# Expert rows gathered on TensorE by one fp32 product per tile in place of two products with split rows

## The reference, cut to what matters

```python
h2 = rmsnorm(x, norm2_g) * (1.0 + scale2) + shift2
# router: softmax over 16 experts, best group of 4, best two experts in it
combine = ...                                   # (tokens, 16), two nonzero per token
hidden = silu(einsum('td,edf->tef', h2, w_gate)) * einsum('td,edf->tef', h2, w_up)
hidden = hidden * combine[:, :, None]
x = x + gate2 * einsum('tef,efd->td', hidden, w_down)
```

## Time and profile before

| | |
|---|---|
| median of 3 runs | 897.79 us (896.08 to 898.65) |
| profiled execution, its own time | 893.21 us |
| its span in the trace | 891.4 us |
| PE busy | 803.2 us (90%) |
| DVE busy | 614.2 us (69%) |
| ACT busy | 432.1 us (48%) |
| DMA, mean over the span | 196 GB/s |

### The profile page before, as it was taken

How to read it: one execution, slowest core, us unless ns; L and a number is a source line. 1 busy time by engine, 2 the same in 40 slices (tenths; PEclk the granted TensorE clock), 3 DMA queues, 4 the chain that set the end, 5 groups by cost and what they waited for, 6 DMA issues and landing times.

```text
span 891.4 us, 10532 instructions
## 1 busy us (share of the span) xinstructions
PE 803.2 (90%) x3988; PEld 640.1 (72%) x3988; DVE 614.2 (69%) x739; ACT 432.1 (48%) x504; POOL 73.3 (8%) x67
## 2 busy tenths in 40 slices
PE   1239999999999979999999759999999999999993
PEld 0028878787666646667888758888888888888882
DVE  3685895122699986553654863979788888888882
ACT  1323214245655545556221634656657575756660
POOL 4020000000000000000000000011111121111111
PEclk9959999999999999999999758999999999999998
DMA  9918958020111131132273251989898989989873
GB/s 317 332 55 323 344 192 314 0 77 19 48 41 56 47 95 48 48 133 81 95 261 142 92 201 60 326 266 347 313 343 309 348 293 328 313 310 336 308 240 51
DMA packets 74809, 174.94 MB, mean 196 GB/s; under 512 B 7272, under 2 KB 16584, under 8 KB 71696
## 3 DMA queue, kind: packets, MB, share of 16 engines
q1 hardware_dynamic: 69712, 156.81, 48.7%
q0 software_dynamic: 5056, 17.59, 8.0%
HBM read 163.86 MB, written 10.52 MB: 196 GB/s over the span
## 4 chain that ended last, share of the span: by engine, by line
PE 83%; DVE 7%; DMA 4%; ACT 2%; issue 1%; POOL 1%; SPq 0%; POOLq 0%; DVEq 0%; ACTq 0%
PE ps L581 21%; PE ps L583 20%; PE ps L582 20%; PE ps L902 7%; PE ps L699 4%; DMA raw<-in_w_ada 2%; DVE acc L1378 1%; PE ps L681 1%; PE ps L783 1%; PE ps L799 1%; PE ps L811 1%; DMA acc<-in_b_ada 1%; PE ps L714 1%; PE ps L727 1%; PE ps L951 1%
## 5 line engine op out<-in xcount | busy, mean ns | idle before, releaser
L1646 DVE TENSOR_TENSOR w_lo<-raw,w_hi 128x2048 fp32r<-128x2048 f32 x96 | 216.9, 2286 | 23.1 <-ACT w_hi L1284 22.5
L1284 ACT ACTIVATE w_hi<-raw 128x2048 fp32r<-128x2048 f32 x96 | 181.8, 1913 | 15.9 <-PE ps L583 15.9
L1368 DVE TENSOR_TENSOR w_lo<-raw,w_hi 128x2048 fp32r<-128x2048 f32 (+1 forms) x28 | 62.1, 2218 | 71.7 <-ACT w_hi L1018 71.4
L581 PE MATMUL ps<-act_lo,w_hi 128*128 128x512 f32 x232 | 98.3, 424 | 8.8 <-DVE w_lo L1368 7.8
L581 PE MATMUL ps<-w_lo,hgT_hi 128*128 128x512 f32 x256 | 101.0, 395 | 0.0
L582 PE MATMUL ps<-w_hi,hgT_lo 128*128 128x512 f32 x256 | 99.8, 390 | 0.0
L583 PE MATMUL ps<-w_hi,hgT_hi 128*128 128x512 f32 x256 | 99.7, 389 | 0.0
L583 PE MATMUL ps<-act_hi,w_hi 128*128 128x512 f32 x232 | 91.6, 395 | 0.0
L582 PE MATMUL ps<-act_hi,w_lo 128*128 128x512 f32 x232 | 91.3, 394 | 0.0
L1018 ACT ACTIVATE w_hi<-raw 128x2048 fp32r<-128x2048 f32 (+1 forms) x28 | 51.8, 1855 | 80.3 <-DMA raw<-in_w_in 43.9
L560 POOL DMA_INDIRECT out<-ys,slot_tok x16 | 49.0, 3061 | 320.3 <-DVE ys L1742 246.2
(11 more groups left out here) (244 smaller groups left out, 1448.6 us busy)
## 6 DMA issues: line engine op xcount, KB each, us to landing
raw<-in_w_gate SPq DMA_DIRECT2D x32, 1024.0 KB, 8.5
raw<-in_w_up SPq DMA_DIRECT2D x32, 1024.0 KB, 6.4
raw<-in_w_down SPq DMA_DIRECT2D x32, 1024.0 KB, 8.7
raw<-in_w_ada SPq DMA_DIRECT2D x24, 1024.0 KB, 7.1
raw<-in_w_in SPq DMA_DIRECT2D x18, 1024.0 KB, 6.4
raw<-in_w_out SPq DMA_DIRECT2D x4, 1024.0 KB, 5.0
xres<-in_x SPq DMA_DIRECT2D x1, 2048.0 KB, 17.9
raw<-in_w_o_a SPq DMA_DIRECT2D x2, 1024.0 KB, 5.0
```

The source lines that it names most:

```text
L581: pe.matmul(o, a[0], b[1], start=start, stop=False)
L1284: act.activation(e_hi[s_][:, :], e_raw[r][:, :], ACT.Copy).then_inc(e_top, 1)
L1368: dve.tensor_tensor(lo, r, hi.bitcast(F32), ALU.subtract).then_inc(chunk_split, 1)
L1646: dve.tensor_tensor(e_lo[s_][:, :], e_raw[r][:, :], e_hi[s_][:, :].bitcast(F32), ALU.subtract).then_inc(e_split, 1)
```

## The change

The gather takes the fp32 rows `h2f` themselves as stationary operand, and `sel` as fp32, in one plain fp32 product in place of two fp32r ones. `h2_hi` and `h2_lo` are not made any more. Since `h2f` must now live through the experts, what lay on it (`ys`, `hid`, `hidT_hi`, `hidT_lo`, `gate2`) moves to where the split rows were. `sel` being fp32, `slot_t` becomes fp32 too and has two columns (number, weight). The load of `gate2` waits for the end of `wo1` in place of the split rows and the turned rows.

```diff
-    h2_hi = act_hi[:, :, :].rearrange("p k s -> p (k s)").rearrange("p (t d) -> p t d", t=NT)
-    h2_lo = act_lo[:, :, :].rearrange("p k s -> p (k s)").rearrange("p (t d) -> p t d", t=NT)
...
-    ys = [at(f"ys{i}", [D], F32, 160 + 4 * i) for i in range(2)]
-    sel = at("sel", [NT, 2, P], F32R, 168)
+    ys = [at(f"ys{i}", [D], F32, 80 + 4 * i) for i in range(2)]
+    sel = at("sel", [NT, 2, P], F32, 168)
     silu = at("silu", [F_EXP], F32, 172)
-    hid = at("hid", [F_EXP], F32, 178)
-    hidT_hi = at("hidT_hi", [4, P], F32R, 180)
-    hidT_lo = at("hidT_lo", [4, P], F32R, 182)
-    gate2 = at("gate2", [D], F32, 174)
+    hid = at("hid", [F_EXP], F32, 92)
+    hidT_hi = at("hidT_hi", [4, P], F32R, 94)
+    hidT_lo = at("hidT_lo", [4, P], F32R, 96)
+    gate2 = at("gate2", [D], F32, 88)
...
-    slot_t = at("slot_t", [NT, N_EXP, 4], F32R, 185)
+    slot_t = at("slot_t", [NT, N_EXP, 2], F32, 185)
...
 # POOL, after the four stores of xres
-            pool.wait_ge(h2_sp, NT)
-            pool.wait_ge(h2T_ps, 2 * NT)
+            pool.wait_ge(seg_ready, seg_done("wo1", 3))
             pool.dma_start(gate2[:, :], mod_d[1][:, D:2 * D]...).then_inc(ld_g2, 16)
...
 # TensorE, gather and slot_table
                         for tt in range(NT):
-                            for n, part in enumerate((h2_hi, h2_lo)):
-                                last = pe.matmul(ps[2 + u % 2][:, 2 * P * (kk % 2):2 * P * (kk % 2) + 2 * P],
-                                                 part[:, tt, P * kk:P * kk + P], sel[:, tt, :, :],
-                                                 start=(tt == 0 and n == 0), stop=(tt == NT - 1 and n == 1))
+                            last = pe.matmul(ps[2 + u % 2][:, 2 * P * (kk % 2):2 * P * (kk % 2) + 2 * P],
+                                             h2f[tt][:, P * kk:P * kk + P],
+                                             sel[:, tt, :, :].rearrange("p b s -> p (b s)"),
+                                             start=(tt == 0), stop=(tt == NT - 1))
...
-                        last = pe.matmul(ps[7][:, 4 * b:4 * b + 4], sel[:, tt, b, :],
+                        last = pe.matmul(ps[7][:, 2 * b:2 * b + 2], sel[:, tt, b, :],
                                          slot_t[:, tt, bass.ds(e + b, 1), :].rearrange("p a n -> p (a n)"),
                                          start=(tt == 0), stop=(tt == NT - 1))
...
-            pe.wait_ge(h2_sp, NT)
+            pe.wait_ge(h2_rows, NT)
             expert_pass(0)
...
 # ACT
-            def rows_high(tt):
-                act.wait_ge(h2_rows, tt + 1)
-                if tt == 2:
-
-                    act.wait_ge(seg_ready, seg_done("wo1", 3))
-                act.activation(h2_hi[:, tt, :], h2f[tt][:, :], ACT.Copy).then_inc(h2_hiR, 1)
...
             for tt in range(NT):
-                rows_high(tt)
                 if tt + 2 < NT:
                     mean_square(tt + 2)
...
 # DVE
-            for tt in range(NT):
-                dve.wait_ge(h2_hiR, tt + 1)
-                dve.tensor_tensor(h2_lo[:, tt, :], h2f[tt][:, :], h2_hi[:, tt, :].bitcast(F32), ALU.subtract
-                                  ).then_inc(h2_sp, 1)
...
                 dve.tensor_copy(slot_t[:, :, :, 0], tid[:, :].unsqueeze(2).broadcast_to([P, NT, N_EXP]))
-                link(dve.tensor_copy(slot_t[:, :, :, 1], comb[:, :, :]))
-                dve.tensor_tensor(slot_t[:, :, :, 2], comb[:, :, :], slot_t[:, :, :, 1].bitcast(F32), ALU.subtract
-                                  ).then_inc(tab_ok, 1)
+                dve.tensor_copy(slot_t[:, :, :, 1], comb[:, :, :]).then_inc(tab_ok, 1)
...
-                dve.tensor_copy(slot_tok[:, b:b + 1], ps[7][:, 4 * b:4 * b + 1])
-                dve.tensor_reduce(slot_w[:, b:b + 1], ps[7][:, 4 * b + 1:4 * b + 3], AX.X, ALU.add).then_inc(idx_ok, 1)
+                dve.tensor_copy(slot_tok[:, b:b + 1], ps[7][:, 2 * b:2 * b + 1])
+                dve.tensor_copy(slot_w[:, b:b + 1], ps[7][:, 2 * b + 1:2 * b + 2]).then_inc(idx_ok, 1)
...
-            dve.memset(slot_t[:, :, :, :].bitcast(F32), 0.0)
             expert_pass(0)
```

More of the change, by code:

```diff
@@ L312, in hybrid_layer @@
         merged_ok, m_hi, m_sp = sem("merged_ok"), sem("m_hi"), sem("m_sp")
-        x1_ready, h2_ss, h2_sd, h2_rows, h2_hiR, h2_sp = (
-            sem(n) for n in ("x1_ready", "h2_ss", "h2_sd", "h2_rows", "h2_hi_ready", "h2_split"))
+        x1_ready, h2_ss, h2_sd, h2_rows = (
+            sem(n) for n in ("x1_ready", "h2_ss", "h2_sd", "h2_rows"))
         h2T_ps, h2T_sb, r_ps, r_exp, r_sel, pos_ps, route_ok = (
```

## The result

The changed kernel takes 953.4 us, the median of 4 runs (951.26 to 954.19), against 897.06 us for the kernel before in the same measurement. The ratio is 1.0623, with a 95% interval of 1.0598 to 1.0647. The change makes the kernel 56 us slower. The profiled execution took 954.19 us, its span is 952.4 us.

The account below looks back on a forecast made before the run. TensorE was taken to bound the experts' part. Seven gathers 43.1, first gather 6.3 and slot tables 6.6, less 0.3 for the clearing, gave 55.7 us on 897.8: 953.5 us, range 947 to 961.

Parts of the forecast that it names:

- What bounds it: Experts' part: TensorE never waits, busy 44.00 of 44 us, so time added there comes out at the end.
- A plain fp32 product is two records: Gather: 32 fp32 products still give 64 records, as the router's 32 products give 64.
- The record's price, 0.216 us: Gather at full clock: 0.216 us per 256-column fp32 record, read in the attention, so 13.82 us a gather against 7.66.
- Seven gathers: The gathers in two halves among the experts: 6.16 us more each, 43.1 us in all, bounds 40.5 to 44.9.
- The first gather, +6.3: Ahead of all experts: clock rises 6.1 us after its start, 16.9 us against 10.59, so 6.3 us more.
- The slot table, +6.6: Eight tables: 16 fp32 records of 0.101 us each, 1.62 us against 0.79, 6.6 us more in all.
- the bounds: Slot table's record price: least 0.099 us (fp32r, four columns), most 0.105 (fp32, 128 columns).
- The front, nothing but the clearing of the table: Ahead of the experts: removed ACT copies and DVE subtractions weren't awaited, worth nothing; clearing `slot_t` goes, 0.3 us gained.
- Nothing for the first fp32r product behind the fp32 gather: After each gather: a 0.34 us first step in place of 0.23 taken as nothing, 0.9 us at the upper end.
- The Trainium skill: Gather: its four passes for true fp32 gave an estimate of 42.0 us more for seven; the forecast stayed with 43.1.

Follow-up runs that it names:

- the two runs with one part each: Slot table alone as plain fp32 in the kernel before: 904.21 us; changed kernel with the table back in fp32r, gather alone: 946.29 us.
- the runs with idle products: Unused 512-column products, 16 ahead of the routing's counts and 14 ahead of the first gather: changed kernel 949.46 us, kernel before 893.81 us.

## Why the prediction was right

The forecast was 953.5 us and the median is 953.4. The mechanism held, step by step, but so close a hit is luck: the forecast stood on a median of before of 897.8 us, which is 897.1 in this measurement, and the increase was 56.3 us where 55.7 were forecast. By its own steps:

- **What bounds it.** TensorE was taken for the only limit in the experts' part, and it is: 49.00 of 49 us, and both parts of the change arrive at the end in full (49.3 and 7.2 us). Shown by that window and by the two runs with one part each.
- **A plain fp32 product is two records.** 512 records for 256 products.
- **The record's price, 0.216 us.** Measured 6.91 / 32 = 0.216, a half gather 6.91 us as forecast. That it is the columns and not the load is shown by the run with 128 columns. Seven gathers cost 43.1 us more, the term of the sum to the digit.
- **The first gather, +6.3.** Measured +6.09. Its excess over a warm gather was ascribed to the clock, and the runs with idle products show this for 2.6 of the 2.9 us. The moment at which the clock rises isn't fixed: with the table alone changed, the same fp32r gather takes 10.16 us and not 10.59. So the agreement to 0.2 us is in part luck.
- **The slot table, +6.6.** Measured 8 x 0.89 = 7.1: the one term that was mis-sized, by 0.5 us. A narrow fp32 record takes 0.105 us at full clock and not 0.101. The router's record at half clock, halved, was the wrong choice between the bounds; the fp32 record of 128 columns had the right value.
- **The front, nothing but the clearing of the table.** From the router's first record to the first gather 32.99 us before (502.15 to 535.14) and 32.78 after: 0.2 us less, 0.3 forecast. The clearing of 0.27 us is gone, and `sel` takes 1.21 us in place of 1.15. The run that still makes the split rows shows that they were free.
- **Nothing for the first fp32r product behind the fp32 gather.** Behind the fp32 gather the steps are 0.23 us, and the 0.34 us step stands only behind the slot table, as before. In the distance of the pair shown, 49.22 us, the gathers' +6.16 and the table's +0.89 explain 7.05 of 7.05.
- **The Trainium skill** ("FP8 and Floating Point Precision", TensorE Precision Notes) has true fp32 at four passes, which gave an estimate of 42.0 us more for the seven gathers; the trace has 43.1, so it agrees within 3%. The one pass of a reduced-precision read, which the prediction sets beside it, is not stated there; what the trace has is one record of 0.120 us for an fp32r product of 256 columns. Its "Perfetto Trace Analysis" (Identifying the Most-Contended Engine) calls the busy share of the matmuls a poor measure of how close TensorE is to its roofline, and names two others: MFU, which the prediction left out, and the busy share of the weight loads. That second share is 37.94 of 44 us before and 41.60 of 49 after, 0.86 and 0.85, while a pair became 17% longer. So taken alone, as the prediction took it, the share of the loads doesn't tell which of these two kernels is the slower; MFU wasn't worked out.

The sum of the measured parts is 43.1 + 6.1 + 7.1 - 0.2 = 56.1 us, and the difference of the medians is 56.3. The two traces differ by more, 57.3 us from the router's first record to the end of the span. The rest lies behind the last expert: between the landing of the last scatter and POOL's last work the chain has 0.50 us of "issue" in the trace of before and 2.15 in the one of after. In the other traces that stretch is between 0.50 and 2.53 us, in variants of the kernel before (0.50 to 2.53) as in those of the changed one (0.82 to 2.34), so I don't put it down to the change.

## What to carry to other kernels

One fp32 product for two fp32r ones is no saving on TensorE: it is two records, each with nearly twice the time of an fp32r record of 256 columns (0.216 against 0.120 us), so it costs nearly double, and only at 128 columns, where an fp32r record is hardly shorter (0.110), are the two about equal (3.57 against 3.52 us for a half gather). Before counting the vector work that such a change takes away, look at the idle time behind that work; here 4.6 us of DVE had 5.6 us of idle time after them and were worth nothing. A busy TensorE at 1.2 GHz ahead of a dense part is worth a look: wide idle products in its waits gave 1.1%.

## What the runs showed of the hardware

- TensorE can be busy without a gap and stay at 1.2 GHz. The fp32r gather with 128 columns ran 13.89 us at a granted clock of 0.50, and the clock rose only behind it, among products of 512 columns. The fp32 gather with the same 128 columns had its clock up within its 8.98 us, and with 512-column products around them the router's narrow records ran at 1.00.
- Where every record has its own 128x128 load, narrower products stop getting quicker near 0.1 us a record: 0.099 us for fp32r with 4 columns, 0.105 for fp32 with 2, 0.110 for fp32r with 128, 0.112 for fp32 with 128, all at 2.4 GHz. For fp32r, going from 256 to 128 columns gains only 0.120 - 0.110. At 1.2 GHz the least is about double: 0.202 for the router's records (3.23 / 16), 0.217 for fp32r with 128 columns (13.89 / 64). That the load sets this floor is argued and not shown.
- One stretch of the same instructions can lose its clock in one execution and keep it in another. Of the eleven traces, the two with the clock at 1.00 from 330 to 340 us start the router at 502.1 us, the other nine between 504.1 and 506.3, and none of those has 1.00 there. A change of a few us needs many runs to be told from it: the idle products in the kernel before gave 3.9 us in the trace and an interval of the medians that reaches 1.0004. The mean clock helps: by it, 12 of the 25 runs of before were early ones, and if the two of the ten with idle products that have the higher clock (0.964) are early ones too, the gain is 2.5 us among the early and 3.0 among the late.
